# First GEMM of a hybrid decoder layer: norm weights spread by TensorE, a new order of loads and of half-tile steps, softplus moved behind a weight split

## The reference

```
xn = rmsnorm(x, norm1_w);  proj = xn @ w_in      # 1024 -> q, k, v, z, xbc, dt, gates
dt = softplus(dt_raw + dt_bias)
attn = window attention with sinks (q, k, v) @ w_attn_o
ssd  = Mamba-2 scan over conv'd xbc, gated by silu(z), group norm, @ w_ssd_o
h = x + (gate_a*attn + gate_s*ssd) @ w_out
h = h + (silu(gt)*val) @ w_down,  (val, gt) = conv(rmsnorm(h, norm2_w) @ w_up)
out = rmsnorm(h, final_norm_w)
```

## Time and profile before

| | us |
|---|---|
| timed runs, median (lowest to highest) | 1051.74 (1051.51 to 1052.51) |
| the profiled execution's own time | 1054.41 |
| span of the profiled execution, first to last instruction | 1052.7 |
| TensorE (PE) busy | 1025.8 |
| VectorE (DVE) busy | 674.9 |
| ScalarE (ACT) busy | 450.8 |
| GpSimd (POOL) busy | 135.9 |
| mean granted TensorE clock | 0.996 |

### The profile page before, as it was taken

The page is one execution under the profiler, slowest core; times in us unless marked ns, Lnnn a source line. Parts: engine busy times, 40 slices in busy tenths (PEclk is TensorE's granted clock), DMA queues, the critical chain, the costliest instruction groups (busy, mean ns, idle before and its releaser), DMA issues.

```text
span 1052.7 us, 13318 instructions
## 1 busy us (share of the span) xinstructions
PE 1025.8 (97%) x4983; PEld 834.4 (79%) x4983; DVE 674.9 (64%) x918; ACT 450.8 (43%) x843; POOL 135.9 (13%) x134
## 2 busy tenths in 40 slices
PE   6999999999999899999999999999999999999997
PEld 6877777777787787878788888898888888888886
DVE  4537998785687786898774444557766666651323
ACT  6235656453445444546452221344444444431132
POOL 3001110111443310224420110000000000000000
PEclk9999999999999999999999999999999999999999
DMA  7622112225556233454435644133233223233222
GB/s 224 124 89 80 63 60 79 81 81 129 146 131 156 85 116 101 130 134 143 124 113 169 230 130 150 40 102 99 86 113 115 84 80 101 81 139 99 86 74 80
DMA packets 123641, 117.01 MB, mean 111 GB/s; under 512 B 21357, under 2 KB 111797, under 8 KB 123589
## 3 DMA queue, kind: packets, MB, share of 16 engines
q1 hardware_dynamic: 95653, 95.26, 28.9%
q10 hardware_dynamic: 25344, 12.59, 4.9%
q0 software_dynamic: 2592, 8.46, 2.2%
HBM read 109.93 MB, written 6.36 MB: 110 GB/s over the span
## 4 chain that ended last, share of the span: by engine, by line
PE 75%; DVE 14%; issue 6%; ACT 2%; POOL 1%; DMA 1%; ACTq 0%; DVEq 0%; SPq 0%; POOLq 0%
PE banks L1177 24%; PE banks L1178 23%; PE banks L1179 23%; DVE conv_acc L1125 3%; DVE w_lo L830 3%; PE banks L1223 1%; PE banks L1275 1%; PE banks L1243 1%; ACT probs L610 1%; POOL xs L553 1%; PE banks L1190 1%; DMA x_nat<-in_x 1%; DVE small L908 1%; DVE scores L905 1%; DVE decay L961 1%
## 5 line engine op out<-in xcount | busy, mean ns | idle before, releaser
L830 DVE TENSOR_TENSOR w_lo<-w_raw,w_hi 128x1024 fp32r<-128x1024 f32 (+1 forms) x166 | 200.1, 1245 | 110.2 <-ACT w_hi L576 108.9
L576 ACT ACTIVATE w_hi<-w_raw 128x1024 fp32r<-128x1024 f32 (+1 forms) x170 | 166.7, 1029 | 115.5 <-PE banks L1179 107.6
L1177 PE MATMUL banks<-xn_hi,w_hi 128*128 128x512 f32 x528 | 215.0, 407 | 0.7 <-DVE w_lo L830 0.5
L1178 PE MATMUL banks<-xn_lo,w_hi 128*128 128x512 f32 x528 | 206.6, 391 | 0.0
L1179 PE MATMUL banks<-xn_hi,w_lo 128*128 128x512 f32 x528 | 206.3, 391 | 0.0
L1177 PE MATMUL banks<-hn_hi,w_hi 128*128 128x512 f32 (+1 forms) x384 | 142.8, 372 | 0.0
L1178 PE MATMUL banks<-hn_lo,w_hi 128*128 128x512 f32 (+1 forms) x384 | 142.6, 371 | 0.0
L1179 PE MATMUL banks<-hn_hi,w_lo 128*128 128x512 f32 (+1 forms) x384 | 142.6, 371 | 0.0
L1177 PEld LDWEIGHTS banks<-xn_hi,w_hi 128*128 128x128 f32 x528 | 99.5, 188 | 32.0 <-issue 11.8
L1179 PEld LDWEIGHTS banks<-xn_hi,w_lo 128*128 128x128 f32 x528 | 99.3, 188 | 21.9
L1178 PEld LDWEIGHTS banks<-xn_lo,w_hi 128*128 128x128 f32 x528 | 99.6, 189 | 19.5 <-issue 1.0
(11 more groups left out here) (205 smaller groups left out, 1522.8 us busy)
## 6 DMA issues: line engine op xcount, KB each, us to landing
w_raw<-in_w_in SPq DMA_DIRECT2D x29, 1024.0 KB, 5.2
w_raw<-in_w_up SPq DMA_DIRECT2D x22, 1024.0 KB, 5.0
decay<-acs_scratch ACTq DMA_DIRECT2D x16, 512.0 KB, 5.7
w_raw<-in_w_ssd_o SPq DMA_DIRECT2D x8, 1024.0 KB, 5.9
w_raw<-in_w_down SPq DMA_DIRECT2D x8, 1024.0 KB, 4.9
w_raw<-in_w_in SPq DMA_DIRECT2D x16, 256.0 KB, 4.3
w_raw<-in_w_attn_o SPq DMA_DIRECT2D x16, 256.0 KB, 4.6
decay_off<-acs_scratch ACTq DMA_DIRECT2D x32, 128.0 KB, 3.6
```

The lines of the kernel that those rows point to most:

```text
L576: A.activation(whi[:, c % 2, lo_:hi_], raw[:, c % 2, lo_:hi_], ACT.Copy).then_inc(w_rounded, 1)
L830: V.tensor_tensor(wlo[:, c % 2, lo_:hi_], raw[:, c % 2, lo_:hi_], f32(whi[:, c % 2, lo_:hi_]), ALU.subtract).then_inc(w_split, 1)
L1177: T.matmul(out_, w[0], m[0], start=first, stop=False)
L1178: T.matmul(out_, w[0], m[1], start=False, stop=False)
```

## The change

Norm row: it is loaded as one row into one partition, ahead of x. TensorE multiplies a one-partition row of ones by it, 512 columns at a time, into banks 2 and 3, and the scaling reads it there. Ahead of this TensorE does seven, and behind it three, matmuls of the ones tile by itself into bank 0. Loads: norm row, x 0, vd 0, x 1, x 2, x 3, vd 1. Half tiles: scaling, transposes, rounding and remainder are handed over by half a tile (512 channels), in lists written out for each engine. TensorE runs the blocks of the two vd chunks in the order of `VD_ORDER`. The lo part of the vd chunks moves from GpSimd to VectorE. Softplus: its first two operations stay, the chain behind them comes after the split of chunk q 0. The diff, cut to its core (the second norm keeps the old functions with its indices adapted):

```diff
+VD_ORDER = ((0, 0), (0, 1), (0, 2), (1, 0), (1, 1), (0, 3), (1, 2), (1, 3))
+for _k, _ct in enumerate(VD_ORDER):
+    DONE[_ct] = _k + 1
+DONE[0], DONE[1] = DONE[0, 3], DONE[1, 3]
+N1_ORDER = ((0, 0), (1, 0), (0, 1), (2, 0), (1, 1), (2, 1), (3, 0), (3, 1))
+N1_AT = {_th: _k + 1 for _k, _th in enumerate(N1_ORDER)}
...
-        n1row = sb("norm1_row", [P, D], 144)
+        n1row = sb("norm1_row", [1, D], 144)
...
                 if is_loop(*CHUNKS[c]):
                     continue
-                for t in ((0, 1), (2, 3))[c] if c < 2 else ():
+                if c == 0:
+                    eng.dma_start(n1row[:, :], norm1_w[0].unsqueeze(0)).then_inc(n1_in, 16)
+                for t in ((0,), (1, 2, 3))[c] if c < 2 else ():
                     eng.dma_start(xnat[:, t, :], x[0, t * P:(t + 1) * P, :]).then_inc(x_in[t], 16)
-                    if t == 0:
-                        eng.dma_start(n1row[:, :], norm1_w[0].unsqueeze(0).broadcast_to([P, D])).then_inc(n1_in, 16)
...
-            for c in range(2):
-                for k, (lo_, hi_) in enumerate(halves(c)):
-                    eng.wait_ge(w_rounded, 2 * c + k + 1)
-                    eng.tensor_tensor(wlo[:, c % 2, lo_:hi_], raw[:, c % 2, lo_:hi_], f32(whi[:, c % 2, lo_:hi_]),
-                                      ALU.subtract).then_inc(w_split, 1)
...
-            for t in range(NT):
+            def square_x(t):
                 eng.wait_ge(x_in[t], 16)
                 norm_square(t, t, xnat, junk[:, :], ss, sd)
-                if t == 1:
-                    split(0)
-                if t:
-                    norm_round(t - 1, t - 1, xn_hi)
-            split(1)
-            norm_round(NT - 1, NT - 1, xn_hi)
+            def round_x(t, hf):
+                eng.wait_ge(n_tp, 2 * t + hf + 1)
+                A.activation(xn_hi[:, hf * KT // 2:(hf + 1) * KT // 2, t * P:(t + 1) * P],
+                             PS[:, 4 + 2 * (t % 2) + hf, :].rearrange("p (k l) -> p k l", l=P),
+                             ACT.Copy).then_inc(n_hi, 1)
+            def round_w(c, hf):
+                if hf == 0:
+                    eng.wait_ge(w_in_slot[c], loads_before[c])
+                lo_, hi_ = halves(c)[hf]
+                A.activation(whi[:, c, lo_:hi_], raw[:, c, lo_:hi_], ACT.Copy).then_inc(w_rounded, 1)
+            square_x(0)
+            round_w(0, 0)
+            round_w(0, 1)
+            round_x(0, 0)
+            square_x(1)
+            square_x(2)
+            round_x(1, 0)
+            round_x(0, 1)
+            round_x(2, 0)
+            round_w(1, 0)
+            round_x(1, 1)
+            round_w(1, 1)
+            square_x(3)
+            round_x(2, 1)
+            round_x(3, 0)
+            round_x(3, 1)
...
-                if c == 2:
-                    eng.wait_ge(w_split, 4)
...
-            norm_scale(0, 0, xnat, sd, rs, xsc, n1row)
-            for t in range(NT):
-                if t + 1 < NT:
-                    norm_scale(t + 1, t + 1, xnat, sd, rs, xsc, n1row)
-                norm_lo(t, t, xn_hi, xn_lo)
+            def scale_x(t, hf):
+                cols = slice(hf * 512, hf * 512 + 512)
+                if hf == 0:
+                    eng.wait_ge(n_sd, t + 1)
+                    V.reciprocal(rs[:, t:t + 1], sd[:, t:t + 1]).then_inc(n_rs, 1)
+                    eng.wait_ge(n_rs, t + 1)
+                if t == 0:
+                    eng.wait_ge(n1_spread, hf + 1)
+                if t >= 2:
+                    eng.wait_ge(n_tp, 2 * (t - 2) + hf + 1)
+                V.scalar_tensor_tensor(out=xsc[:, t % 2, cols], in0=xnat[:, t, cols], scalar=rs[:, t:t + 1],
+                                       in1=PS[:, 2 + hf, :], op0=ALU.mult, op1=ALU.mult).then_inc(n_sc, 1)
+            def rest_of_x(t, hf):
+                eng.wait_ge(n_hi, N1_AT[t, hf])
+                part = (slice(0, P), slice(hf * KT // 2, (hf + 1) * KT // 2), slice(t * P, (t + 1) * P))
+                V.tensor_tensor(xn_lo[part], PS[:, 4 + 2 * (t % 2) + hf, :].rearrange("p (k l) -> p k l", l=P),
+                                f32(xn_hi[part]), ALU.subtract).then_inc(n_lo, 1)
+            def rest_of_w(c, hf):
+                lo_, hi_ = halves(c)[hf]
+                eng.wait_ge(w_rounded, 2 * c + hf + 1)
+                V.tensor_tensor(wlo[:, c, lo_:hi_], raw[:, c, lo_:hi_], f32(whi[:, c, lo_:hi_]),
+                                ALU.subtract).then_inc(w_split, 1)
+            scale_x(0, 0)
+            scale_x(0, 1)
+            rest_of_w(0, 0)
+            rest_of_x(0, 0)
+            rest_of_w(0, 1)
+            scale_x(1, 0)
+            scale_x(1, 1)
+            scale_x(2, 0)
+            rest_of_x(1, 0)
+            rest_of_x(0, 1)
+            rest_of_x(2, 0)
+            rest_of_w(1, 0)
+            scale_x(2, 1)
+            rest_of_w(1, 1)
+            rest_of_x(1, 1)
+            scale_x(3, 0)
+            rest_of_x(2, 1)
+            scale_x(3, 1)
+            rest_of_x(3, 0)
+            rest_of_x(3, 1)
...
                     V.tensor_tensor(e, X, q_, ALU.max).then_inc(spc, 1)
+                if kind == "k":
                     eng.wait_ge(spa, 2)
...
-            norm_transposes(0, 0, xsc)
-            norm_transposes(1, 1, xsc)
+            def warm(n):
+                for _ in range(n):
+                    T.matmul(PS[:, 0, 0:P], ones[:, :], ones[:, :], start=True, stop=True)
+            def turn_x(t, hf):
+                b = 4 + 2 * (t % 2) + hf
+                eng.wait_ge(n_sc, 2 * t + hf + 1)
+                take(b, n_lo, N1_AT[t, hf])
+                for j in range(4):
+                    kt = 4 * hf + j
+                    ins = T.transpose(PS[:, b, j * P:(j + 1) * P], xsc[:, t % 2, kt * P:(kt + 1) * P], ident[:, :])
+                ins.then_inc(n_tp, 1)
+            def vd_block(c, t):
+                if c == 0:
+                    take(t, v_ready, 2 * (t + 1))
+                eng.wait_ge(n_lo, N1_AT[t, c])
+                tok = slice(t * P, (t + 1) * P)
+                for kt in range(4):
+                    if t == 0 and kt in (0, 2):
+                        eng.wait_ge(w_split, 2 * c + 1 + (kt > 0))
+                    cols_ = slice(kt * VW, (kt + 1) * VW)
+                    ins = three(PS[:, t, 0:VW], (xn_hi[:, 4 * c + kt, tok], xn_lo[:, 4 * c + kt, tok]),
+                                (whi[:, c, cols_], wlo[:, c, cols_]), c == 0 and kt == 0, c == 1 and kt == 3)
+                ins.then_inc(gemm_done, 1)
+            eng.wait_ge(consts, 3)
+            warm(7)
+            eng.wait_ge(n1_in, 16)
+            for hf in range(2):
+                take(2 + hf, n_sc, 2 * (NT - 1) + hf + 1)
+                T.matmul(PS[:, 2 + hf, :], ones[0:1, :], n1row[0:1, hf * 512:hf * 512 + 512], start=True,
+                         stop=True).then_inc(n1_spread, 1)
+            warm(3)
+            eng.wait_ge(consts, 13)
+            turn_x(0, 0)
+            turn_x(0, 1)
+            vd_block(0, 0)
+            turn_x(1, 0)
+            turn_x(1, 1)
+            turn_x(2, 0)
+            vd_block(0, 1)
+            vd_block(0, 2)
+            turn_x(2, 1)
+            vd_block(1, 0)
+            turn_x(3, 0)
+            vd_block(1, 1)
+            turn_x(3, 1)
+            vd_block(0, 3)
+            vd_block(1, 2)
+            vd_block(1, 3)
...
+                if kind == "vd":
+                    if i == 1:
+                        eng.wait_ge(params_in, 16 * len(PARAM_ROWS))
+                        for k, n in enumerate(PARAM_SIZES):
+                            take(4 + k, pcols, 3)
+                            T.transpose(PS[:, 4 + k, 0:n], stage[0:n, k, :], ident[0:n, 0:n]).then_inc(pcols_t, 1)
+                    continue
```

More of the change, by code:

```diff
@@ L297, in sem @@
             return ctx.enter_context(nc.semaphore(name))
-        n1_in, n2_in = sem("norm1_in"), sem("norm2_in")
+        n1_in, n2_in, n1_spread = sem("norm1_in"), sem("norm2_in"), sem("norm1_spread")
         x_in = [sem(f"x_in{t}") for t in range(NT)]
@@ L838, in norm_scale @@
                 if t == 0:
-                    eng.wait_ge(n2_in if k else n1_in, 16)
-                if k >= 2:
-                    eng.wait_ge(n_tp, 2 * (k - 1))
+                    eng.wait_ge(n2_in, 16)
+                eng.wait_ge(n_tp, 2 * (k - 1))
                 V.scalar_tensor_tensor(out=dst[:, t % 2, :], in0=src[:, t, :], scalar=inv[:, t:t + 1], in1=row[:, :],
@@ L1182, in norm_transposes @@
                 b = 4 + 2 * (t % 2)
-                if k == 0:
-                    eng.wait_ge(consts, 13)
-                eng.wait_ge(n_sc, k + 1)
+                eng.wait_ge(n_sc, NT + k + 1)
                 for hf in range(2):
@@ L1332, in _ @@
                     continue
-                if kind in FORM_B:
-                    if kind == "vd":
-                        nk, width, k0, first, last = 4, VW, 4 * i, i == 0, i == 1
-                        mh, ml, b0 = xn_hi, xn_lo, 0
-                        took, per = v_ready, 2
-                    elif kind == "out":
```

(21 more changed lines are left out.)

## The result

The changed kernel took 1057.34 us (median of 10 runs, 1054.67 to 1060.17), the kernel before beside it 1052.84: ratio 1.0037, 95% interval 1.0023 to 1.0051. By the ratio it is slower by some 3.9 us. I forecast 1052.9 and no change, with a range up to 1055.4.

What follows compares the result with a forecast made beforehand. TensorE, busy 97% of the span, was taken as the bound. GEMM -1.0, clock +1.8, hand-over +0.85 and softplus -0.52 summed to +1.1 us on a median of 1051.74: forecast 1052.9 us, range 1050.0 to 1055.4.

Steps and rivals of the forecast that it cites:

- the clock in the matmuls on constants: Start of TensorE's work: the matmuls on constants raise the clock at 5.3 us, or at 9.9 at the latest.
- second rival: Front up to chunk k: clock slow throughout, GEMM ends at 31.8 to 32.8 us, time 1054.8 us; chance 0.14.
- Early start: Start of the GEMM: norm row spread by 6.6 us, first block at 9.2 rather than 12.73, 3.5 us gained there.
- Bank wait: Before block (0,2): TensorE idles from 14.5 to 17.75 us for scaling (3,0); GEMM ends only 1.0 us earlier.
- third rival: Before block (0,2): the bank wait does not bite, GEMM ends at 25.2 to 26 us, time 1048 us; chance 0.16.
- Clock in the hole: TensorE idle before block (0,2): the clock falls, 3.6 us at half speed, +1.8 us (bounds 0 and +2.2).
- Hand-over to chunk k: Between GEMM and chunk k: TensorE waits for the first v copy to free bank 0, +0.85 us.
- Softplus: Before chunk q 0: moving the softplus chain behind the split removes the wait there, -0.52 us.
- Base: Whole kernel: the forecast was put on the kernel before's timed median of 1051.74 us.

Runs made afterwards that it cites:

- b_constants: Kernel before with 14 full-height matmuls of the ones tile ahead of its first transposes: 1052.58 us, ratio 0.9993.
- a_no_constants: Changed kernel without its 7 and 3 matmuls on constants: 1055.48 us, ratio 1.0024.
- b_one_row_constants: Kernel before with 14 matmuls using one partition of the ones tile ahead of its first transposes: 1052.50 us, ratio 0.9994.
- a_row_in_sbuf: Changed kernel with full-height spread, x tile 0 first, two v copies ahead of chunk k's split, norm row copied from PSUM to SBUF: 1049.43 us, ratio 0.9966.
- a_softplus_back: Changed kernel with the softplus chain back ahead of the split of chunk q 0: 1058.28 us, ratio 1.0060.
- b_softplus_moved: Kernel before with the softplus chain moved behind the split of chunk q 0, nothing else: 1051.28 us, ratio 0.9987.
- a_fill_hole: Changed kernel with ten more matmuls on constants in TensorE's idle time before block (0,2): 1056.96 us, ratio 1.0046.
- a0_again: The changed kernel unaltered, timed and traced a second time, against the kernel before: 1055.97 us, ratio 1.0028.

## Why the prediction was wrong

The step that failed is the clock in the matmuls on constants: "I take 5.3, since these are matmuls", with 9.9 as the other end. In the first trace the rise came near 5 us. In the second, after 8.6 us of nothing but matmuls (7 full-height, the one-row spread, 3 full-height), it had still not come, and it came only behind the GEMM's first block, near 16.5. My second rival had the mechanism, with too small a chance (0.14) and too small a price: its GEMM ends at 31.8 to 32.8, the late kind's at 34.85, and that costs +5.3 us at 63 us, not +3.

The one-row spread is the cause that the experiments support. By the durations, the six traces with full-height constants and a one-row spread show the rise near 5 us three times and near 16.5 three times. The four with full height throughout (b_constants and the three with the full-height spread) show it by 7 us each time; the two with one-row matmuls alone show it only near 13.5 and 17 (a_no_constants, b_one_row_constants). And of 29 executions with a full-height spread one lies above its group, by 2 us, where 13 of the 22 of the changed kernel lie in the upper group. That is support and not proof: an execution without a trace does not tell where its clock rose, and what makes the mixed start come out early or late stays open.

The other terms:

- *Early start.* Spread done 6.6 (measured 6.59), first block 9.2 (9.58). Right, in one kind of execution.
- *Bank wait.* Hole of 3.25 us from 14.5 (2.79 from 16.0), block (0,2) at 17.75 (18.80). Right; a_row_in_sbuf shows it by taking its cause away. The third rival, that it would not bite, was wrong.
- *Clock in the hole.* +1.8: the fall is shown, its price is 1.3 to 1.6 (12.3 to 12.5 us behind the hole against 10.98). It fell in all six traces with a hole of 2.8 to 3.1 us, and in none of the three with a wait of 0.9 us or none in its place, nor in the filled one. I had left out that it can fall a first time at 8.2, between the constants and the first block. a_softplus_back, where it did not, reaches the parameter transposes 0.63 us earlier; that is most of the 0.8 us by which the GEMM ended later than I said (31.1 for 30.3).
- *Hand-over to chunk k.* +0.85. The idle time is 0.55; from the parameter transposes to chunk k it is 1.00 where it was 0.24, so +0.76. Right.
- *Softplus.* -0.52, the idle time alone. From chunk k to 63 us the lag shrank by 0.74 us (2.37 to 1.63), and by 0.77 in b_softplus_moved. Right in kind, somewhat small. So the early kind is +1.61 (end of the GEMM) + 0.76 - 0.74 = +1.63, where I had summed +1.1.
- *Base.* I put the change on 1051.74, a median of three. Beside the changed kernel the kernel before took 1052.84: 1.1 us of the miss has nothing to do with the change. The trace that I summed on has a span of 1052.7, when the median is 1050.9, and two traces of this program differ by up to 1.6 us for every fall of the clock that one has and the other has not.
- *Outside the span.* 2.12 us instead of 1.74: not foreseen, 0.38, not settled.

How far this goes, as an estimate: the first trace's lag of 1.63 us at 63 us and the second's of 5.34 give 3.5 if half of the executions are late, and with the 0.38 that is the 3.9 of the ratio. Of the 4.4 us by which 1057.34 lies above 1052.9, the front has 2.4 beyond the forecast, the time outside the span 0.38 and the base 1.1. The half is taken from six traces. By their spans seven of the ten executions behind the 1057.34 lie in the upper group, and six of the twelve in the repeat, whose ratio is 1.0028. The remaining 0.6 us stays open.

## What to carry to other kernels

When a tile borrows a PSUM bank, look for the last reader before the bank's next writer: here the seventh of eight half-tile scalings stood in front of the third of eight blocks, and the cure was either to put other work in front of that block or to copy the tile out. A start that depends on the clock has more than one length; take several traces before you add up terms of half a microsecond. Here matmuls made to raise the clock did so every time only where they were full in height up to the first transposes.

## What the runs showed of the hardware

Matmuls of one partition and the same columns did not raise TensorE's clock where those of 128 partitions did (6.33 against 4.80 us for 28 passes). A fall of the clock lasted some 3.4 us (once 6.8, from 7.7 to 14.5 us in a_fill_hole); behind the hole it cost 1.3 to 1.6 us. The length of an idle time alone did not decide it: 2.79 us in the first trace led to a fall, 2.57 us at 367 us in b_one_row_constants did not (the sixteen decay matmuls behind it took 1.09 us), and 2.58 us before the same matmuls in b_constants did (1.97 us). The clock column reads 1.00 in the slow start of an execution, before its first recorded change (12 to 16 us in a0_again, where 12 matmuls of 288 columns took 3.0 us), so a mean of 0.998 can belong to the slower run. The Trainium skill (TensorE: Matmul & The Clock Gate, Part 1: The HAM clock gate) says that the transition comes up to half a microsecond earlier or later from one run to the next. These traces agree that it varies, and not on the size: near 5 and near 16.5 us for the same program.
